# RWKV role preparation inside the gate tiles of the input projection, in units of 256 tokens, and gate stores issued by ScalarE

## What is computed

```python
proj = hn @ w_in[l]
gates = jax.nn.sigmoid(proj[..., RWKV_PROJ + S5_WIDTH:])
p = p + (_token_shift(p) - p) * mu
r, k, v, wd, ad, gd = jnp.split(p, RWKV_SPLITS, axis=-1)
w_log = -jax.nn.softplus(-(w0 + jnp.tanh(wd) @ w_up)) - 0.5
decay = jnp.exp(-jnp.exp(w_log.astype(f32)))
a = jax.nn.sigmoid(a0 + ad @ a_up)
g = jax.nn.sigmoid(gd) @ g_up
kk = kk / jnp.maximum(jnp.linalg.norm(kk, axis=-1, keepdims=True), 1e-12)
k = k * (1 + (a - 1) * k_a)
bonus = jnp.sum(r_h * k_h * r_k.astype(f32), axis=-1, keepdims=True) * v_h
```

## Time and profile before

| | us |
|---|---|
| median of 3 runs | 3407.45 (3406.24 to 3410.00) |
| profiled execution, its own time | 3410.13 |
| its span, first to last instruction | 3408.3 |
| TensorE busy in the span | 3186.7 (93%) |
| VectorE busy | 1785.2 (52%) |
| ScalarE busy | 1211.6 (36%) |
| GpSimd busy | 121.6 (4%) |

### The profile page before, as it was taken

The page is one execution under the profiler, slowest core; times in us unless marked ns, Lnnn a source line. Parts: engine busy times, 40 slices in busy tenths (PEclk is TensorE's granted clock), DMA queues, the critical chain, the costliest instruction groups (busy, mean ns, idle before and its releaser), DMA issues. The chain is left out here.

```text
span 3408.3 us, 67757 instructions
## 1 busy us (share of the span) xinstructions
PE 3186.7 (93%) x25690; PEld 2826.8 (83%) x25690; DVE 1785.2 (52%) x3179; ACT 1211.6 (36%) x1937; POOL 121.6 (4%) x126
## 2 busy tenths in 40 slices
PE   8999999999875888869999989999999999899998
PEld 7989999999754777759998868999988888688887
DVE  7666642222295566645435557666786666311333
ACT  6211123343373344433113335444554444312211
POOL 0000000000000222220000000000000000000000
PEclk9999999999876999989999989999999999999999
DMA  5333344334474333424336733323432221411442
GB/s 159 100 138 127 115 139 129 119 119 128 156 280 148 81 89 89 98 83 157 115 109 195 218 125 102 109 99 105 141 106 90 82 77 67 153 51 49 143 125 87
DMA packets 350699, 409.20 MB, mean 120 GB/s; under 512 B 137184, under 2 KB 280416, under 8 KB 344592
## 3 DMA queue, kind: packets, MB, share of 16 engines
q1 hardware_dynamic: 350608, 407.99, 38.0%
HBM read 260.31 MB, written 147.59 MB: 120 GB/s over the span
## 5 line engine op out<-in xcount | busy, mean ns | idle before, releaser
L434 PE MATMUL psum<-x_hi,proj_w_hi 128*128 128x416 f32 (+1 forms) x1280 | 457.6, 358 | 0.0
L434 PE MATMUL psum<-x_hi,proj_w_lo 128*128 128x416 f32 (+1 forms) x1280 | 447.4, 350 | 0.0
L434 PE MATMUL psum<-x_lo,proj_w_hi 128*128 128x416 f32 (+1 forms) x1280 | 447.2, 349 | 0.0
L2678 PE MATMUL psum<-up_x,up_w_hi 128*128 128x512 f32 (+2 forms) x1540 | 352.0, 350 | 12.4 <-ACT up_w_hi L2699 6.7
L2684 PE MATMUL psum<-up_x,up_w_hi 128*128 128x512 f32 (+2 forms) x1540 | 352.2, 350 | 1.3 <-DVE up_x L2836 1.3
L2681 PE MATMUL psum<-up_x,up_w_lo 128*128 128x512 f32 (+2 forms) x1540 | 350.7, 350 | 0.0
L2678 PEld LDWEIGHTS psum<-up_x,up_w_hi 128*128 128x128 f32 x1540 | 259.0, 189 | 53.9 <-issue 6.8
L2684 PEld LDWEIGHTS psum<-up_x,up_w_hi 128*128 128x128 f32 x1540 | 259.1, 189 | 42.2 <-DVE up_x L2836 2.0
L2681 PEld LDWEIGHTS psum<-up_x,up_w_lo 128*128 128x128 f32 x1540 | 259.1, 189 | 40.6
L2305 PE MATMUL psum<-down_w_hi,down_a_hi 128*128 128x512 f32 x704 | 274.7, 390 | 13.4 <-DVE down_w_lo L2464 12.6
L2305 PE MATMUL psum<-down_w_hi,down_a_lo 128*128 128x512 f32 x704 | 274.4, 390 | 0.0
(11 more groups left out here) (347 smaller groups left out, 5667.9 us busy)
## 6 DMA issues: line engine op xcount, KB each, us to landing
scratch_hidden<-up_hidden SPq DMA_DIRECT2D x44, 512.0 KB, 2.6
down_a_raw<-scratch_hidden SPq DMA_DIRECT2D x32, 704.0 KB, 6.1
up_weight<-in_w_up_sets SPq DMA_DIRECT2D x42, 512.0 KB, 4.5
up_weight<-in_w_up_sets SPq DMA_DIRECT2D x84, 256.0 KB, 3.3
proj_area<-scratch_s_tab SPq DMA_DIRECT2D x32, 608.5 KB, 3.8
scratch_s_tab<-proj_area SPq DMA_DIRECT2D x16, 1089.0 KB, 4.3
proj_weight<-in_w_in_tiles SPq DMA_DIRECT2D x33, 512.0 KB, 4.1
scratch_gates<-proj_mixed SPq DMA_DIRECT2D x16, 1032.0 KB, 4.0
```

The source lines that it names most:

```text
L434: mm = nc.tensor.matmul(psum[:, PRODUCT_BANKS[n], 0:WIDTHS[n]], w[:, v, k, :], x[:, k, block_of(n)], start=(k == 0 and w is w_hi and x is ...
L2678: nc.tensor.matmul(out, w_hi[:, q % 7, k, :], x_hi(phase, step)[:, k, cols], start=opens and k == 0, stop=False, skip_group_check=True)
```

## The change

`rwkv_prepare` is gone. Its arithmetic stands in the gate tiles, in 32 units of 256 tokens (the first of each pair has the 16 meta tokens too, 272): two units a tile, called even and odd, four tiles a span of tokens, all pairs of it. Unit s has t = s // 2, the tile's number. TensorE does the five products of a unit (`sum_w`, `sum_a`, `sum_norm`, `sum_g`, `sum_bonus`) one by one after every half block of the gate products, in banks 3 and 7; the gate blocks use banks 0, 1 and 2 in turn. The exponentials, the roles and the bonus of the odd unit are done in the next tile, those of the last one in a tail. The fields of a unit (r, key, v, the decay and the roles) lie in one buffer for even and one for odd units, and r and key of the next unit of that kind are loaded once the roles of the last are stored. The gate row is one buffer, and ScalarE evicts a block into it, waits for its own eviction and issues the store of that block; SP issues no gate store. y of the S5 branch is held once instead of twice. The two tiles of low rank channels come first of the RWKV tiles. The last y of S5 and the last roles count on one semaphore, for which the chunk stage waits before it loads its second group.

```diff
+            def load_rk(s, t, span, q, j, n, first):
+                after(sp, roles_stored[q], 16 * t)
+                sp.dma_start(fields[q][:, R_AT:KK_AT + 1, 0:n],
+                             rwkv_out[2 + j:2 + 2 * PAIRS:PAIRS, :, tokens_of(span, first)].rearrange("a p t -> p a t")).then_inc(rk_loaded[q], 16)
...
+            def store_roles(s, t, span, q, j, n, first):
+                sp.wait_ge(role_r, s + 1)
+                sp.wait_ge(role_k, s + 1)
+                sp.wait_ge(role_a, s + 1)
+                sp.wait_ge(role_b, s + 1)
+                sp.dma_start(roles_out[ROLE_A:ROLE_R + 1, j, :, tokens_of(span, first)].rearrange("r p t -> p r t"), fields[q][:, A_AT:R_AT + 1, 0:n]).then_inc(
+                    last_stored if isinstance(s, int) and s == LAST_UNIT else roles_stored[q], 16)
...
+            def gate_tile(m, i, v):
+                t = m - FIRST_GATE
+                even, odd = unit_of(m, i, v, EVEN), unit_of(m, i, v, ODD)
+                if not is_first(m):
+                    odd_done = odd_before(m, i, v)
+                    load_group(2 * t + 1, 1)
+                    if v == 0:
+                        sp.wait_ge(g_summed, 2 * t)
+                        load_gate_low(even[2], SPAN, False)
+                    load_rk(*even)
+                    load_v(*even)
+                    store_g(*odd_done)
+                load(m + 2)
+                if not is_first(m):
+                    store_y(t - 1, 1, y_stored[1])
+                    store_bonus(*odd_done)
+                if not is_first(m):
+                    store_roles(*odd_done)
+                load_rk(*odd)
+                load_v(*odd)
+                store_g(*even)
+                if not is_last(m):
                     load_group(2 * t + 2, 0)
-                    load_group(2 * t + 3, 1)
-                    store_y(t, v, 0)
-                    store_gate(m, v)
-                    if not (isinstance(m, int) and m == TILES - 1):
-                        store_y(t, v, 1)
+                store_y(t, 0, y_stored[0])
+                store_bonus(*even)
+                if v == 1 and not is_last(m):
+                    sp.wait_ge(a_summed, 2 * t + 2)
+                    load_decay_low(even[2] + 1, SPAN, False)
+                store_roles(*even)
 
             def scan_begins():
...
+                first_unit = unit_of(FIRST_GATE, RWKV_END, 0, EVEN)
+                sp.wait_ge(stored[0], 16 * M_RWKV // 2 + 16)
+                sp.wait_ge(stored[1], 16 * M_RWKV // 2)
+                load_decay_low(0, WIDEST, True)
+                load_rk(*first_unit)
+                load_gate_low(0, WIDEST, True)
+                store_rwkv(FIRST_GATE - 1, 1)
+                sp.dma_start(ups, lora).then_inc(ups_loaded, 16)
+                load_v(*first_unit)
...
                 for w in range(TWO):
                     load_group(w, w)
-                store_rwkv(FIRST_GATE - 1, 1)
-            tile_loop(sp, tile, scan_begins)
-            sp.wait_ge(stored[0], 16 * (M_RWKV + M_GATE) // 2 + 16)
-            sp.wait_ge(y_stored[0], 16 * TWO * C * BUILDS // 2 + 16)
...
-                    if kind == "gate" and n == INJECT_AT:
-                        inject(2 * t, 0, t)
-                    if kind == "gate" and n == OUTPUT_AT:
-                        outputs(2 * t, 0)
-                        inject(2 * t + 1, 1, t)
...
+            def sum_a(s, t, span, q, j, n, first):
+                pe.wait_ge(sig_ready, s + 1)
+                nc.tensor.matmul(psum[:, ROLE_BANKS[q], 0:n], ups[64:128, 0, j * P:(j + 1) * P], decay_low[64:128, 0:n], start=True, stop=True).then_inc(a_summed, 1)
...
+                    if h == 0:
+                        sum_w(*even)
+                    if h == 1:
+                        sum_bonus(*odd_before(m, i, v))
+                    if h == 2:
+                        sum_a(*even)
+                    if h == 3:
+                        sum_norm(*even)
+                    if h == 4:
+                        sum_g(*even)
+                    if h == 5:
+                        sum_w(*odd)
+                    if h == 6:
+                        sum_bonus(*even)
+                    if h == 7:
+                        sum_a(*odd)
+                    if h == 8:
+                        sum_norm(*odd)
+                    if h == 9:
+                        sum_g(*odd)
+
...
+                for n in range(NB):
+                    sp.wait_ge(row_stored[n], 16 * M_GATE)
+                for q in (EVEN, ODD):
+                    sp.wait_ge(g_stored[q], 16 * M_GATE)
+                    sp.wait_ge(bonus_stored[q], 16 * M_GATE)
+                    sp.wait_ge(roles_stored[q], 16 * M_GATE - 16 * q)
+                    sp.wait_ge(y_stored[q], 16 * C * (M_GATE - q))
+            tile_loop(sp, tile, scan_begins, gate_tile, tail)
 
         @block.tensor
...
+                        if k == KD // 2 - 1:
+                            half(2 * n)
+                    mm.then_inc(products_done, 1)
+                    half(2 * n + 1)
+                outputs(2 * t + 1, 1)
...
+            def gate_block(m, n):
+                act.wait_ge(products_done, (m + SLOTS) * NB + n + 1)
+                after(act, row_stored[n], 16 * (m - FIRST_GATE))
+                nc.scalar.activation(gate_row[:, block_of(n)], psum[:, GATE_BANKS[n], 0:WIDTHS[n]], ACT.Sigmoid).then_inc(evacuated, 1)
+                act.wait_ge(evacuated, m * NB + NB + n + 1)
+                nc.scalar.dma_start(gate_out[bass.ds(m - FIRST_GATE, 1), :, block_of(n)].rearrange("o p t -> p (o t)"), gate_row[:, block_of(n)]).then_inc(row_stored[n], 16)
...
+                split(m + 1, 1 - v)
...
+                sigmoid_of_w(*even)
+                if not is_first(m):
+                    gelu(t - 1, 1)
+                    exponentials(*odd_before(m, i, v))
+                squared_key(*even)
+                nc.scalar.preload_act_table_set("sigmoid_and_others")
...
+                gate_block(m, 0)
+                if v == 0:
+                    gate_low_sigmoid(even[2], even[5])
+                sigmoid_of_a(*even)
+                gate_block(m, 1)
...
+                gate_block(m, 2)
...
+                sigmoid_of_w(*odd)
...
+                gelu(t, 0)
+                exponentials(*even)
+                squared_key(*odd)
+                nc.scalar.preload_act_table_set("sigmoid_and_others")
+                gate_block(m, 3)
+                sigmoid_of_a(*odd)
+                gate_block(m, 4)
+                copy_of_g(*odd)
+                if v == 1 and not is_last(m):
+                    decay_low_tanh(even[2] + 1, SPAN)
...
+                cumulate(*even)
+                if not is_first(m):
+                    bonus_of(*odd_before(m, i, v))
+                    roles_of(*odd_before(m, i, v))
+                scan(2 * t, 0)
+                key_of(*even)
+                cap_norm(*even)
+                cumulate(*odd)
+                scan(2 * t + 1, 1)
+                bonus_of(*even)
+                roles_of(*even)
+                key_of(*odd)
+                cap_norm(*odd)
 
...
-            rwkv_prepare(nc, "prep", sems, psum, rwkv_proj, ins["lora"], cols, roles, bonus, rwkv_gate, decay, store_last_y, stores_under_way,
-                         last_roles_stored)
+                    ins["w_in_tiles"], cols[:, COL["mu"]:COL["mu"] + M_RWKV], ins["s5_small"], ins["s5_bc"], s5_tab, s5_u, s5_y, rwkv_proj, gates, ident, pre,
+                    ins["lora"], cols, roles, bonus, rwkv_gate, decay, last_roles_stored)
+            stage_ends([last_roles_stored])
```

581 lines of the change are left out of this document (284 added, 297 removed).

## The result

| | us |
|---|---|
| before, median of 4 runs | 3408.72 (3406.24 to 3414.15) |
| changed kernel, median of 4 runs | 3367.97 (3363.24 to 3371.28) |
| ratio | 0.9877, 95% interval 0.986 to 0.9895 |
| profiled execution of the changed kernel | 3363.24, span 3361.4 |

The kernel is 40.8 us faster, 1.2%. The forecast was 3340 in a range of 3320 to 3372, so the sign held and the time lies in the range, near its upper end, but only six tenths of the gain came.

What follows compares the result with a forecast made beforehand. The prediction took TensorE's matmuls to bound the gate tiles and an engine-to-engine chain the preparation. From 3410.1, less 146.9 (seam), plus 68.8 (sums) and 10 (first tile), came 3342.0, put at 3340 us for the median, range 3320 to 3372.

Steps and rivals of the forecast that it cites:

- What bounds the kernel, and the seam: Gate tiles last as long as their matmuls; the 165.98 us preparation becomes a 19.1 us gap, gaining 146.9 us.
- What TensorE takes on: Gate tiles: 160 sums at 0.43 us each add 68.8 us, a tile going from 26.8 to 31.1 us.
- no charge for changing over: Gate-tile sums: inject and outputs matmuls both gave 0.43 us for one, with nothing extra for switching between matmuls.
- The upper bound, 76 us: Gate-tile sums: the preparation's 0.66 us each at clock 0.72, so 0.47 at full clock, 76 us in all.
- (a): Odd unit's roles, store then reload: this DMA round trip becomes the bound, 107 us more, 3447 us; chance 0.05 in full.
- the mild form of (a): Odd unit's DMA round trip at twice the row values: a microsecond a tile, 3355 us; chance 0.07.
- Waits in steady tiles: Steady gate tiles: TensorE waits 0 us, with ScalarE 2.0 us to spare in the even unit, 2.7 in the odd.
- The prediction's estimate by the 2.7 us: Steady gate tiles: table-set loads at that budget would cost some 3.5 us a tile, 56 in all; not in the sum.
- The first tile: First gate tile: late S5 table loads and a wait for the sigmoid of a add 10 us, range 6 to 15.
- an idle of that length costs little clock: First gate tile: TensorE's 6.4 to 10.4 us of idle would hardly lower its granted clock afterwards.
- ScalarE (b): Gate tiles: ScalarE falls behind if a store issue costs it 4.3 us, 53 us more, 3393 us; chance 0.05.
- The fast chunk start (c): Chunk stage: it begins on a fast clock, its first 48 us becoming some 34, 3326 us; chance 0.08.

Runs made afterwards that it cites:

- the run with the tables first: Against the changed kernel, SP issues the S5 tables of groups 0 and 1 ahead of the last RWKV row's store, lora weights and v: 3358.76 us.
- the second experiment: Against the changed kernel, each sum of 64 rows is issued twice in a row with the same operands and bank: 3393.9 us, one run.

## Where the prediction was right, and where it failed

**What bounds the kernel, and the seam.** Right. The gap is 17.6 instead of 19.1. The eight y stores started 0.5 us earlier than laid out (3.1 us behind the last product for 3.6) and took 3.63 and not 4.68. Behind them the order came as laid out: from the issue of the bonus to the first DMA of the next stage 4.0 us for 4.5, and from there to the first matmul 6.9 for 6.3.

**What TensorE takes on: the term that was mis-sized.** 160 x 0.43 = 68.8 stood in the sum; measured are 16 x (32.69 - 26.82) = 93.9, where 26.82 is 429.05 / 16, the mean tile before. The columns, the count and the price of a sum of 128 rows were right. The step that failed is "the rows nearest to them are the inject and outputs matmuls" together with "no charge for changing over": the earlier trace rows are of 128 rows and show nothing of what a change of rows costs, and 64 of the 160 sums have 64. The diff says so (`ups[64:128, ...]`, `decay_low[64:128, ...]`). The upper bound, 76 us, was taken from the mean of the old preparation, where the w and a products stood in runs of four of their kind (the earlier trace rows give only their mean over all five kinds), so a change came at most once for four of them. A bound from a row of another form is no bound. The longer steps at 942.23 in the trace of the kernel before were in reach and are in none of the rows. So is the rule of the Trainium skill, TensorEngine Tiling (Array Packing), "Key Properties", on changes of mode; it speaks against this part of the change, which moves single matmuls of 64 rows between others. That the time still lies in the range is luck: 93.9 is far above this term's own bound of 76, and the room for it came from the 15 us that the range allowed for the mild form of (a), which did not happen.

**Waits in steady tiles.** Right: 0. The rooms were 2.8 (even) and 3.2 (odd unit), forecast 2.0 and 2.7 for a tile 1.6 us shorter; the experiments put the point from which ScalarE decides between 2.57 and 5.13 us of added loads. The load of a table set at 1283 ns, the issue of a store by ScalarE at 0.34 (0.35 was taken) and DMA at 0.55 (0.56) held. ScalarE's 0.61 is below the 0.73 forecast, most of it because its waits for its own evictions do not count as busy and the tile is longer. The prediction's estimate by the 2.7 us of the Trainium skill, ScalarE: Activation LUTs, "Rules for kernel authors", has a slip: 4.25 us less the rooms of 2.0 and 2.7 are 2.25 and 1.55, 3.8 us a tile and 61 in all, not 3.5 and 56; nothing hangs on it.

**The first tile.** The mechanism was right and the run with the tables first shows it. The size was 14.5 for 10: the idle was at the upper end (9.98), the wait for a was 2.0, and "an idle of that length costs little clock" left out most of 2.5 us.

**The rivals.** The round trip (a) was far from binding: 7 us where it decides from about 16.6. The prediction's mild form of it does not follow from its own numbers, since twice 7.0 is 14.0, under the 14.7 from which it would decide, and costs nothing. ScalarE (b) did not fall behind in steady tiles; had it done so, the price would have been above the 53 us, which left out what waits do to the clock (59.5 us of waits cost 96). The fast chunk start (c) did not happen: in 1024 to 1072 the clock was 0.70 against 0.58 before, and the stage was shorter, which the prediction named as its sign, but by 7.1 us and not 14, and most of that is within what kernels with the same code there differ by. When the stage did begin at full clock, in the kernel kept busy, the time was no better.

**Sum.** 3340 + 25.1 (the sums) + 4.5 (the first tile) - 1.5 (the seam) = 3368.1; measured 3367.97. The 7 us of the chunk stage are not in it: they belong to an execution that itself lies 4.7 below the median. That the sum meets the median to 0.1 us is luck, since its terms are read from one execution each and the chunk stage alone varies by more than 5 us between traces.

## What to carry to other kernels

Before costing a matmul by a neighbour's row, look at its rows as well as its columns: a single 64-row matmul between 128-row ones pays for two changes. Filling its weights with zeros to 128 rows takes that away (24.8 us here). Putting those of 64 rows side by side makes them share one visit, as the pairs of the second experiment do; no kernel here was ordered that way. Where TensorE is full, see which loads a queue puts behind a store that waits for its data. A wait in a dense stretch costs more than its row says, and more again where the granted clock falls with it.

## What the runs showed of the hardware that was not expected

- Going from 128 to 64 rows and back costs 0.40 us around an fp32 matmul of 256 columns; the matmul itself takes 0.43 with 64 rows as with 128. At each change the next weights are not loaded ahead: that load starts 0.27 us behind the start of the product before it on the way in, and together with its product on the way out.
- Two pauses in each tile of 37 to 41 us, mostly of 1.8 to 2.6 us, came with a granted clock of 0.91 to 0.98 instead of 1.00, and 59.5 us of waits cost 96.
- Three loads of table sets between two activations took 3.88 us, 1.29 each.
- TensorE kept busy up to the chunk stage did not keep its clock: 3 to 8 us into the stage it was 0.60, with TensorE busy 2.41 of 5 us.
- The same code took 45.3 to 50.5 us in its first stretch, from kernel to kernel.
